# Attention's ends, the merged tiles' parts and the row sum inverses, in a two-block transformer kernel on one core

## The reference, cut to what matters

```python
h = modulate(rms_norm(x, norm1[l]), sh1, sc1)          # and the same of the context
na_q, na_k, na_v, gq, gk, gv, ga, gb = split(h @ w_in[l])
# 8 heads of 64: local windows + context keys, with a bias; 8 query heads over 2 key heads: all keys
p = softmax(q @ k.T * SCALE (+ bias));  y = p @ v       # ya (local heads), yb (grouped heads)
merged = sigmoid(ga) * (ya @ w_pa) + sigmoid(gb) * (yb @ w_pb)
x = x + g1 * (merged @ w_o)
x = x + g2 * swiglu(modulate(rms_norm(x, norm2[l]), sh2, sc2))
```

## Time and profile before

| | |
|---|---|
| time, median of 3 runs | 2972.27 us (2970.26 to 2973.64) |
| time of the profiled execution | 2973.45 us |
| its span | 2971.6 us, 40419 instructions |
| mean granted TensorE clock | 0.984 |
| DVE, ACT, POOL busy | 34%, 32%, 28% |
| chain that ended last | PE 80%, issue 8%, DVE 4%, POOL 3%, ACT 3% |

### The profile page before, as it was taken

One profiled execution on the slowest core, in us unless ns is written; L12 is line 12 of the kernel. 1 busy time (PEld: TensorE's weight loads), 2 busy tenths in 40 slices (PEclk: granted clock), 3 DMA queues, 4 the chain that ended last, 5 costly groups with the idle time before them and its releaser, 6 DMA issues.

```text
span 2971.6 us, 40419 instructions
## 1 busy us (share of the span) xinstructions
PE 2877.8 (97%) x16220; PEld 2148.6 (72%) x16220; DVE 1016.7 (34%) x1437; ACT 963.9 (32%) x1671; POOL 829.1 (28%) x648
## 2 busy tenths in 40 slices
PE   8999999999999999999999999999999999999998
PEld 6886778888888888878777777888854644444446
DVE  3507761123111111151474123212377432322325
ACT  3225551124221122242554234222365331212216
POOL 2323223334222322443323444444420400000003
PEclk8999999999999999999999999999999999999999
DMA  5114321111211211212332222232220369999991
GB/s 214 57 68 162 127 93 65 64 52 56 71 53 59 69 68 48 73 57 82 132 111 70 97 89 88 81 110 95 96 77 29 150 271 409 407 400 408 400 375 54
DMA packets 60679, 407.53 MB, mean 137 GB/s; under 512 B 7008, under 2 KB 7408, under 8 KB 16528
## 3 DMA queue, kind: packets, MB, share of 16 engines
q1 hardware_dynamic: 58400, 397.96, 35.9%
q0 software_dynamic: 1872, 6.72, 0.6%
q10 hardware_dynamic: 288, 1.17, 0.1%
HBM read 403.73 MB, written 2.10 MB: 137 GB/s over the span
## 4 chain that ended last, share of the span: by engine, by line
PE 80%; issue 8%; DVE 4%; POOL 3%; ACT 3%; DMA 1%; SPq 0%; POOLq 0%; DVEq 0%; ACTq 0%
PE ps L652 46%; PE ps L1204 8%; PE ps L1227 4%; POOL half_slots L1841 3%; PE ps L892 3%; PE ps L873 3%; PE ps L919 3%; PE ps L1246 2%; PE ps L683 2%; PE ps L1170 2%; PE ps L662 2%; PE ps L1282 1%; PE ps L697 1%; PE ps L923 1%; PE ps L1059 1%
## 5 line engine op out<-in xcount | busy, mean ns | idle before, releaser
L652 PE MATMUL ps<-h_parts,half_slots 128*128 128x512 f32 (+1 forms) x5520 | 1066.1, 355 | 15.3 <-POOL half_slots L1841 14.9
L652 PEld LDWEIGHTS ps<-h_parts,half_slots 128*128 128x128 f32 x5520 | 905.7, 189 | 173.4 <-issue 14.1
L1841 POOL TENSOR_TENSOR half_slots<-ring,half_slots 128x1024 fp32r<-128x1024 f32 (+3 forms) x276 | 593.0, 2149 | 1094.7 <-ACT half_slots L1348 1094.3
L1348 ACT ACTIVATE half_slots<-ring 128x1024 fp32r<-128x1024 f32 (+3 forms) x276 | 263.7, 956 | 1248.9 <-PE ps L652 1236.7
L652 PE MATMUL ps<-hidden_parts,half_slots 128*128 128x512 f32 (+1 forms) x1584 | 305.1, 355 | 0.0
L652 PEld LDWEIGHTS ps<-hidden_parts,half_slots 128*128 128x128 f32 x1584 | 261.0, 188 | 43.6
L652 PE MATMUL ps<-y_parts,half_slots 128*128 128x512 f32 (+1 forms) x1152 | 229.7, 360 | 9.9 <-DVE y_parts L2197 9.7
L652 PEld LDWEIGHTS ps<-y_parts,half_slots 128*128 128x128 f32 x1152 | 193.3, 192 | 44.3 <-issue 11.7
L1204 PE MATMUL ps<-second_block,scratch 128*64 128x512 f32 x1024 | 223.3, 594 | 2.0 <-ACT scratch L1740 1.4
L2250 DVE TENSOR_TENSOR first_block<-ps,first_block 128x768 f32<-128x768 f32 (+1 forms) x44 | 36.3, 825 | 426.8 <-PE ps L652 413.3
L1204 PEld LDWEIGHTS ps<-second_block,scratch 128*64 128x64 f32 x1024 | 74.6, 137 | 143.3 <-issue 143.3
(11 more groups left out here) (348 smaller groups left out, 3211.5 us busy)
## 6 DMA issues: line engine op xcount, KB each, us to landing
second_block<-experts SPq DMA_DIRECT2D x192, 1024.0 KB, 9.0
ring<-stream SPq DMA_DIRECT2D x138, 1024.0 KB, 4.9
ring<-stream SPq DMA_DIRECT2D x16, 768.0 KB, 4.2
ring<-stream SPq DMA_DIRECT2D x16, 640.0 KB, 3.9
ring<-stream SPq DMA_DIRECT2D x16, 512.0 KB, 3.7
mod_head_low<-stream SPq DMA_DIRECT2D x6, 1024.0 KB, 19.5
first_block<-bias POOLq DMA_DIRECT2D x16, 384.0 KB, 4.8
second_block<-w_gate SPq DMA_DIRECT2D x4, 1024.0 KB, 6.0
```

The lines of the kernel that those rows point to most:

```text
L652: last = nc.tensor.matmul(ps[s % 2][:, a:b], part(x, s)[:, k, :], parts[y][:, tile + k, a:b], start=start and k == 0 and n == 0, stop=stop ...
L1348: act.activation(part(0, s), raw_half(s), ACT.Copy).then_inc(hi_done, 1)
L1841: nc.gpsimd.tensor_tensor(part(1, s), raw_half(s), part(0, s).bitcast(fp32), ALU.subtract)\
```

## The change

- At the start of attention PE makes the first scores before it turns the last value features, and waits for these only in the second pass of the loop. For that `upper_k(0)` on ACT stands before the last value features are kept (it waits for the product before the last one), and POOL's first query parts wait only for the queries.
- In the last pairs ACT makes the upper parts of the first two merge halves, and POOL the lower part of the first; the lower part of the second comes when all scores are made.
- `MS2` is now `HS`. The fourth round of merge is written out in the ACT and DVE programs, and beside its last two products the parts of M tiles 0 to 3 and 4 to 5 are made. Tiles 6 and 7 come after.
- The reciprocal is of two columns, into `small[:, 2]`, with no wait for the product before; each of two products takes one column, broadcast over 64 columns, as its weights, and writes 64 partitions. The tile `inverses` goes, `rb` gets its own.

```diff
-        MS2 = YS2
+        MS2 = HS
...  tensor (PE)
-                turn_v(4, nav + 3)
...
-                    nc.tensor.matmul(ps[3][:, at + P:at + 2 * P], inverses[:, :], ident, start=True,
-                                     stop=True).then_inc(s_pv, 1)
+                    for half in range(2):
+                        one = (2 * g + half) % 8
+                        last = nc.tensor.matmul(ps[3][half * HD:(half + 1) * HD, at + P:at + 2 * P],
+                                                small[:, 2, one:one + 1].to_broadcast([P, HD]), ident,
+                                                start=True, stop=True)
+                    last.then_inc(s_pv, 1)
...
-                pe.wait_ge(v_k, 5 * (l + 1))
+                scores(0)
+                turn_v(4, nav + 3)
                 for i in range(NP + 2):
+                    if i == 1:
+                        pe.wait_ge(v_k, 5 * (l + 1))
...
-                    if i < NP:
+                    if 1 <= i < NP:
                         scores(i)
...  scalar (ACT)
                 for j in range(4):
+                    if j == 3:
+                        act.wait_ge(steps, 2 * SLOT0[l, "mod_rest"] - 1)
+                        upper_k(0)
                     keep_v_features(j + 1, s + j)
...
-                upper_k(0)
...
+                    if i in (NP - 1, NP):
+                        upper(2 * SLOT0[l, "merge"] + i - NP + 1)
...
-                upper(s0)
-                upper(s0 + 1)
                 act.wait_ge(s_y, g0 + NP)
...
+                def upper_merged(tiles):
+                    for k in tiles:
+                        act.wait_ge(merged, 8 * l + k + 1)
+                        act.activation(MS2[0][:, k, 0:nt], M[:, k, 0:nt], ACT.Copy).then_inc(y_hi, 1)
...  in gates(i), ahead of upper(s + 2, 8, i)
+                            if isinstance(i, int) and i == 3 and j == 3:
+                                upper_merged((range(0, 4), range(4, 6))[half])
...
-                with act.Fori(1, 4) as i:
+                with act.Fori(1, 3) as i:
                     gates(i)
-
-                act.wait_ge(steps, 2 * SLOT0[l, "w_o"])
-                for k in range(KD):
-                    act.wait_ge(merged, 8 * l + k + 1)
-                    act.activation(MS2[0][:, k, 0:nt], M[:, k, 0:nt], ACT.Copy).then_inc(y_hi, 1)
+                gates(3)
+                upper_merged(range(6, 8))
...  gpsimd (POOL)
-                pool.wait_ge(evac["A"], evacuated("A", 2 * SLOT0[l, "mod_rest"] - 1))
+                pool.wait_ge(evac["A"], evacuated("A", 2 * SLOT0[l, "nav"] - 1))
...
+                    if i == NP - 1:
+                        lower(2 * SLOT0[l, "merge"])
                 s0 = 2 * SLOT0[l, "merge"]
-                lower(s0)
+                pool.wait_ge(s_sc, 2 * (g0 + NP))
                 lower(s0 + 1)
...  vector (DVE)
-                        if g:
-                            dve.wait_ge(s_pv, g)
-                        nc.vector.reciprocal(inverses.rearrange("p (a n) -> p a n", n=HD),
-                                             small[:, 1, c:c + 2][:, :, None].to_broadcast([P, 2, HD])).then_inc(s_ri, 1)
+                        nc.vector.reciprocal(small[:, 2, c:c + 2], small[:, 1, c:c + 2]).then_inc(s_ri, 1)
...  in products(i), ahead of the multiplication
+                            if isinstance(i, int) and i == 3 and j == 3:
+                                lower_y(MS2, M, 16 * l + 8, (range(0, 4), range(4, 6))[half])
...
-                with dve.Fori(1, 4) as i:
+                with dve.Fori(1, 3) as i:
                     products(i)
-                lower_y(MS2, M, 16 * l + 8)
+                products(3)
+                lower_y(MS2, M, 16 * l + 8, range(6, 8))
```

More of the change, by code:

```diff
@@ L379, in build @@
         last_ssq, last_rt = small[:, 2, :], small[:, 3, :]
-        inverses = sb("inverses", [P, 2 * HD])
         wslot = sb("wslot", [P, 1])
         WR = view(sc2_rows, 0, KD, NR)
-        rb = sc2_rows[:, KD * NR:KD * NR + NR]
+        rb = sb("rb", [P, NR])
         def token_part(x, c, q):
@@ L1433, in _, with upper_k @@
                 s = 2 * SLOT0[l, "nav"]
+                def upper_k(t):
+                    src = KNA[:, t, :] if t < 4 else KG[:, 0, :]
+                    act.activation(KU[:, t, :], src, ACT.Copy).then_inc(k_hi, 1)
                 for j in range(4):
+                    if j == 3:
+                        act.wait_ge(steps, 2 * SLOT0[l, "mod_rest"] - 1)
+                        upper_k(0)
                     keep_v_features(j + 1, s + j)
@@ L1444, in _ @@
                 slot = SLOT0[l, "mod_rest"]
-                def upper_k(t):
-                    src = KNA[:, t, :] if t < 4 else KG[:, 0, :]
-                    act.activation(KU[:, t, :], src, ACT.Copy).then_inc(k_hi, 1)
                 def keep_turned(i, groups):
@@ L2192, in _, with lower_y @@
                 nt = ntq
-                def lower_y(parts, src, first):
-                    for k in range(KD):
+                def lower_y(parts, src, first, tiles=range(KD)):
+                    for k in tiles:
                         dve.wait_ge(y_hi, first + k + 1)
```

## The result

The changed kernel takes 2932.20 us (median of 4 runs, 2930.95 to 2933.91) beside 2972.43 us (4 runs, 2970.26 to 2973.64): a ratio of 0.9863, with a 95% interval from 0.9850 to 0.9877. It is faster by 40.2 us. The profiled execution took 2933.91 us with a span of 2932.1, against a span of 2971.6 before, so the two traces differ by 39.5 us.

What follows compares the result with a forecast made beforehand. PE, busy 97% of the span, was taken as the bound, so only its work or holes counted. Terms 4.3 + 3.4 + 5.4 + 5.2 + 7.8 + 4.4 = 30.5 us gave 2942 us, range 2933 to 2957.

Steps and rivals of the forecast that it cites:

- Start of attention: Before the first scores: scores go ahead of the last value turning, gaining 4.3 us in layer 0, 3.4 in layer 1.
- End of attention: Before the first merge product: parts made in the last pairs gain 5.4 us in layer 0, 5.2 in layer 1.
- Merge to w_o: Before the first w_o product: parts made beside merge's last products gain 7.8 us in layer 0, 4.4 in layer 1.
- Half clock: Behind the holes at three seams per layer: half clock costs 13.3 us in all and goes with the holes.
- The first rival: At the seams: holes shrink but half clock comes behind them as before; 13.3 us stay, 2955 us; chance 15%.
- Inverses: In attention's pairs: two products of 64 columns change nothing on PE (0); DVE's freed time, up to 60 us, almost all off-path.
- I keep -5: Lower bound on the inverses' PE products: -16 us if nothing but 0.26 us counts, kept as -5.
- the second rival: Middle of attention: the freed DVE shortens it too, 5 to 8 us more, 2935 us; chance 12%.
- Two products one after the other: In attention's pairs: each of four records takes as long as an old one, 39 us more, 2981 us; chance 4%.

Runs made afterwards that it cites:

- late_start: The changed kernel with the start of attention as before: 2945.00 us, ratio 0.9908.
- both_further: The changed kernel with the exp table asked for early and DVE's lower parts of tiles 4 and 5 behind the last addition: 2933.20 us, ratio 0.9865.
- late_merge: The changed kernel with the parts of merge's first two halves made after the last pair, as before: 2944.74 us, ratio 0.9904.
- merged_after: The changed kernel with the merged tiles' parts made after the last product, as before: 2949.92 us, ratio 0.9918.
- filled_hole: The kernel before, with 18 products that nothing needs in the hole before w_o: 2969.62 us, ratio 0.9989.
- wide_reciprocal: The changed kernel with DVE's old 128x128 reciprocal and its wait, but two products of 64 columns from it: 2933.24 us, ratio 0.9869.
- old_inverses: The changed kernel with the old inverses (128x128 reciprocal with its wait, one product of 128 columns): median 2941.9 us, ratio 0.9896.
- inverses_alone: The kernel before with only the new inverses (two-column reciprocal, two products of 64 columns): 2964.96 us, ratio 0.9974.

## Why the prediction was short, step by step

- **Start of attention**: right in mechanism and size, 8.4 us of 7.7. late_start gives back 8.4. In layer 0 the third pair's scores start at 231.28 against 234.92 in the earlier trace rows, though the turning ahead of them came 1.0 later. The table load was late next, as foreseen: without it 1.4 us per layer more would have come (both_further).
- **End of attention**: right, 10.3 us of 10.6 (late_merge). Layer 0's hole is 0.51 us, 0.7 foreseen; in layer 1 there is none.
- **Merge to w_o**: right in layer 0, short in layer 1; 11.3 us of 12.2 for both by merged_after. Layer 1's hole is 1.36 us, 1.8 foreseen, but the term left out the waits of 0.32 and 0.87 us behind it. The prediction saw contention between DVE and POOL as a longer POOL. What came was a DVE that stands: its addition, begun during POOL's subtraction, ends 0.55 us after it and so takes 2.16 us instead of 0.69, and the lower parts behind it are late.
- **Half clock**: right. No seam of the six falls in the two traces of the changed kernel, late_start, late_merge and merged_after bring each fall back with its hole, and filled_hole takes one away alone, for 2.8 us where 3.1 was foreseen and 1.7 where 1.7 was. The first rival falls. A closed hole does not rule the fall out, though: wide_reciprocal has the same start and had half clock there in layer 0, for 0.25 us to the third pair's scores and 1.2 behind them.
- **Inverses**: this step failed. The prediction said "no change" and "I take 0" for PE's products, and for DVE's freed time "almost none of it on the path". Measured are 8.0 us (old_inverses), 8.2 (inverses_alone), 8.3 (the two traces). Of these some 7.1 are PE's products (the 5.8 of inverses_alone's expectation leave the half clock in wide_reciprocal out). The prediction compared the length of two groups of records, 0.49 and 0.26 plus a tail, and that was right: the product is no shorter. It did not look at the gap ahead of it, [0.17 <-issue] in the row of the old product's loads, nor at the tile in the rows on both sides. Even the bound on this term, "I keep -5", was passed. The other 1.0 us is DVE's, nearly all in layer 0. So the second rival had an eighth of it in mechanism, and it is luck that its time, 2935, came nearest.
- **Two products one after the other** (the slower rival): wrong. Four records take 0.39 us on PE.
- **Untouched code**: no term foresaw it. It gave 1.4 us net in the profiled execution. The second block, same code in every kernel, took 798.6 us before, 793.9 after and 793.9 again; in the nine other kernels of the experiments it took 792.6 to 799.2.

The second block's difference is half clock. Here is the same place, 225 us into that block, in the kernel before and in the changed one:

```profile
2398.00:2412.00 14.00, 9.55 (x34) 6.73 (x34) 3.38 (x7) 5.38 (x14) 0.00 (x0) 0.76 0.01 2
```

```profile
2363.00:2377.00 14.00, 9.48 (x49) 5.73 (x50) 3.23 (x8) 6.23 (x12) 0.00 (x0) 1.00 0.00 0
```

PE is busy for 9.55 and 9.48 us of 14 and issues 34 and 49 products: nearly the same busy time, at a mean clock of 0.76 and of 1.00. Whether such a place falls is thus not read from its own hole. The sum of the change's own stretches by undoing each is 8.4 + 10.3 + 11.3 + 8.0 = 38.0 us, as in the table. By medians the four undoings cost 12.8, 12.5, 17.7 and 9.7 us, 52.7 together and more than the whole change, so medians can't be added up here. What the second block adds, some 4.6 us of the 40.2, is left open: the changed kernel showed it twice, but an execution of late_start, the kernel's lowest of four, had it too (793.3 us) beside others up to 6.8 us longer whose traces were not taken. No run tells whether it comes with the time at which the block starts or by chance.

With the inverses at 8.0 us the sum of the prediction would have been 38.5 us and its time 2934; the rest is within what the second block moves.

## What to carry to other kernels

When one product is exchanged for two smaller ones, read the array tile in the rows before and behind them and count the changes between neighbours, since a group's busy time does not hold the gap ahead of it. Take a hole in PE together with the half clock behind it, which here was some 30 to 60% of what closing it gave (1.5 of 5.1 us for the end of attention in layer 1, 2.6 of 4.6 for the start in layer 0), but look at the low-busy seams further on too, because half clock stood there in some executions and not in others, whatever had been closed. An operation that is made beside another engine's is to be priced by the row of that pairing, and by which of the two begins first, and not by its own row alone.

## What the hardware showed beyond what was expected

- A change of the array tile from one PE instruction to the next (128*64, 128*128, 128*32, 64*128) costs 0.20 us: 0.42 against 0.22 us from the inverses' loads to the next instruction's, and 0.31 against 0.10 us from the weighting's last load to them. It was paid 30 times less, for 6.0 of the 7.1 us. The Trainium skill, TensorEngine Tiling (Array Packing), section Key Properties, says that changing the tiling mode, and not just the tile, drains TensorE. The trace agrees that a change costs time, 0.20 us each; that it is a drain no run here shows.
- Column tiles of the same rows do overlap. A record of 128*64 counts 0.053 us in a group of 16 loads (0.85 / 16) and 0.064 in one of 24, where one load takes 0.137 us and one product 0.273, so loads lie beside running products. The Trainium skill, TensorE: Matmul & The Clock Gate, section The mechanism, says that a load overlaps a running matmul only when the row groups differ; this case's rows do not agree, with four records of the two halves inside 0.39 us.
- A DVE addition of two SBUF tiles that begins while POOL subtracts takes 2.16 to 2.19 us and ends 0.55 (512 columns) or 0.81 us (768) after the subtraction; the same takes 0.69 or 0.96 alone, and 0.69 beside POOL if one input is in PSUM. The Trainium skill, GPSIMD Engine Reference, section Specifications, says that both share an interface and contend for instructions of two SBUF inputs. The trace agrees, and shows that the one which began first keeps its pace while the other stands: POOL took 2.38 us at 1701.65, before DVE's addition of 1702.42, and 3.15 in the earlier trace rows, where DVE's addition of 0.96 us had begun 0.06 us before it.
- Half clock comes and goes in a seam of unchanged code: the seam from w_o to ffn had a mean clock of 1.00 in the kernel before, 0.86 in filled_hole and in inverses_alone, and 0.93 and 1.00 in two executions of the changed kernel (700 to 724 us). Filling a hole won 2.8 us before w_o in layer 0, and 2.2 were lost in that seam; whether the one brought the other is open.
